# Second layer's x: from TensorE's 128x128 transposes to VectorE's 32x32 blocks and scattering transfers

## What is computed

```
def hybrid_layer(x, w_in, a_group_w, a_scale, b_sinks, c_rel_bias, w_out, ln_gain, ln_bias):
    h = jnp.einsum('bsd,de->bse', x, w_in)
    a_v, a_gate, b_q, b_k, b_v, b_gate, c_q, c_k, c_v, c_gate = jnp.split(h, _split_points(), axis=-1)
    a_out = pool_mixer(a_v, a_group_w, a_scale) * jax.nn.silu(a_gate)
    b_out = swa_sink_attention(b_q, b_k, b_v, b_sinks) * jax.nn.silu(b_gate)
    c_out = chunk_relbias_attention(c_q, c_k, c_v, c_rel_bias) * jax.nn.silu(c_gate)
    mix = jnp.concatenate([a_out, b_out, c_out], axis=-1)
    y = jnp.einsum('bse,ed->bsd', mix, w_out)
    return _layer_norm(DEEPNORM_ALPHA * x + y, ln_gain, ln_bias)

def reference(x, ...):
    for l in range(DEPTH):
        x = hybrid_layer(x, w_in[l], a_group_w[l], ...)
    return x
```

## Time and profile before

| | |
|---|---|
| median of three runs | 2855.98 us |
| the profiled execution's own time | 2856.79 us |
| its span in the profile | 2854.9 us |
| TensorE (PE) busy | 2833.2 us, 99% |
| VectorE (DVE) busy | 1727.1 us, 60% |
| ScalarE (ACT) busy | 1305.9 us, 46% |
| GpSimd (POOL) busy | 1250.3 us, 44% |
| DMA | 364.43 MB, 128 GB/s in the mean |

### The profile page before, as it was taken

The page is one execution under the profiler, slowest core; times in us unless marked ns, Lnnn a source line. Parts: engine busy times, 40 slices in busy tenths (PEclk is TensorE's granted clock), DMA queues, the critical chain, the costliest instruction groups (busy, mean ns, idle before and its releaser), DMA issues.

```text
span 2854.9 us, 45183 instructions
## 1 busy us (share of the span) xinstructions
PE 2833.2 (99%) x13520; PEld 2373.2 (83%) x13520; DVE 1727.1 (60%) x2898; ACT 1305.9 (46%) x2711; POOL 1250.3 (44%) x926
## 2 busy tenths in 40 slices
PE   8999999999999999999999999999999999999998
PEld 7888888888888888888888888888888888888886
DVE  5555579623666777861166666895127667678624
ACT  4444466523444445652244444664234444456521
POOL 4444444444344434444444444444444444444441
PEclk9999999999999999999999999999999999999999
DMA  6333222355444422235554443224454444222442
GB/s 197 123 122 122 94 86 83 103 175 182 143 144 143 144 85 86 88 98 168 167 167 152 148 148 95 84 82 137 145 180 138 141 144 143 86 85 81 137 156 103
DMA packets 189168, 364.43 MB, mean 128 GB/s; under 512 B 18912, under 2 KB 27136, under 8 KB 185344
## 3 DMA queue, kind: packets, MB, share of 16 engines
q1 hardware_dynamic: 185264, 347.25, 38.2%
q10 hardware_dynamic: 3792, 15.73, 1.4%
HBM read 320.94 MB, written 45.11 MB: 128 GB/s over the span
## 4 chain that ended last, share of the span: by engine, by line
PE 99%; DVE 0%; DMA 0%; SPq 0%; issue 0%; ACT 0%; POOL 0%; POOLq 0%
PE acc L555 69%; PE sc L555 17%; PE pv L555 9%; PE sc L616 2%; PE sc L653 1%; PE sc L579 0%; PE acc L585 0%; DMA raw<-in_wall 0%; PE acc L579 0%; PE sc L591 0%; PE pv L579 0%; DVE last_sums L1777 0%; DVE last_sums L1776 0%; SPq L419 0%; POOL wl L1289 0%
## 5 line engine op out<-in xcount | busy, mean ns | idle before, releaser
L1289 POOL TENSOR_TENSOR wl<-raw,wh 128x512 fp32r<-128x512 f32 x920 | 1249.6, 1361 | 1560.8 <-ACT wh L914 1557.9
L555 PE MATMUL acc<-xh,wh 128*128 128x512 f32 x2624 | 1036.8, 395 | 9.6 <-DVE xl L1322 9.6
L914 ACT ACTIVATE wh<-raw 128x512 fp32r<-128x512 f32 x920 | 575.4, 630 | 1020.1 <-PE acc L555 696.0
L555 PE MATMUL acc<-xh,wl 128*128 128x512 f32 x2624 | 1024.6, 390 | 0.0
L555 PE MATMUL acc<-xl,wh 128*128 128x512 f32 x2624 | 1024.4, 390 | 0.0
L555 PEld LDWEIGHTS acc<-xh,wh 128*128 128x128 f32 x2624 | 494.3, 188 | 105.2 <-issue 6.6
L555 PEld LDWEIGHTS acc<-xh,wl 128*128 128x128 f32 x2624 | 493.5, 188 | 105.6
L555 PEld LDWEIGHTS acc<-xl,wh 128*128 128x128 f32 x2624 | 494.8, 189 | 94.4
L555 PE MATMUL sc<-wh,mixh 128*128 128x512 f32 x496 | 195.2, 394 | 0.1
L555 PE MATMUL sc<-wh,mixl 128*128 128x512 f32 x496 | 193.2, 390 | 0.0
L555 PE MATMUL sc<-wl,mixh 128*128 128x512 f32 x496 | 193.0, 389 | 0.0
(11 more groups left out here) (227 smaller groups left out, 3568.8 us busy)
## 6 DMA issues: line engine op xcount, KB each, us to landing
raw<-in_wall SPq DMA_DIRECT2D x920, 256.0 KB, 2.6
res_scratch<-res ACTq DMA_DIRECT2D x12, 1024.0 KB, 4.3
res<-res_scratch SPq DMA_DIRECT2D x12, 1024.0 KB, 4.9
res<-in_x SPq DMA_DIRECT2D x8, 1024.0 KB, 5.8
x_scratch<-res SPq DMA_DIRECT2D x8, 1024.0 KB, 4.7
prob<-x_scratch SPq DMA_DIRECT2D x32, 256.0 KB, 3.3
res<-x_scratch SPq DMA_DIRECT2D x8, 1024.0 KB, 5.8
hist_scratch<-mixh SPq DMA_DIRECT2D x8, 768.0 KB, 4.5
```

What stands on the lines that cost most here:

```text
L555: return nc.tensor.matmul(o, lhsT, rhs, start=start, stop=stop)
L914: return nc.scalar.activation(o, i, ACT.Copy, scale=scale)
L1289: nc.gpsimd.tensor_tensor(wl[:, s, :], raw[:, s, :], wh[:, s, :].bitcast(F32), ALU.subtract).then_inc(w_lo, 1)
```

## The change

VectorE turns the normalised quarter, still in SBUF, in blocks of 32x32 (`turn_rows`, behind the keys' low parts and ahead of the queries'), into four buffers `turned` that lie over four tiles of `mixh` and `mixl` which only p = 3 fills. SyncE writes these as columns into a new scratch array `x1_t` of 2048 x 1024 (`store_turned`): for each of the units 20 to 23 four transfers ahead of the unit's load, each of 32 partitions x 16 blocks x 32 elements. A run of 32 elements is 128 bytes, and its neighbours in the transfer lie in other rows of `x1_t`. ScalarE waits for all 16 transfers of p before it writes `mixh` behind the last `c_hi`. The plain store into `x1` stays, since the residual is read from it. In the output projections of steps 1 and 2 the pieces are loaded from `x1_t` as step 0 loads them from `x_t`; TensorE's 128 transposes and their waits are gone, and ScalarE and VectorE read `prob` in SBUF.

```diff
+        x1_t = nc.dram_tensor("x1_t_scratch", (D, SEQ), F32, kind="Internal").ap()
...
+        turned = [nc.alloc_sbuf_tensor_at(f"turned{n}", [P, HALF], F32, offset=x_at + 4 * HALF * (at + tile + C_PAIRS - 1))
+                  for n, (at, tile) in enumerate((a, b) for a in (2 * KT, 3 * KT) for b in (MIX_A, MIX_C))]
...
+        def turns(it):
+
+            return 1 <= it <= 2
...
+            sp.sem_inc(turned_out, 16)
...
+            def store_turned(it, n, t):
+
+                sp.wait_ge(turned_ok, n * QT + (16 * it + t + 1))
+                for i in range(4):
+                    at = half(it) * HALF + t * P + 32 * i
+                    sp.dma_start(x1_t.rearrange("(n j a) s -> n a j s", n=4, a=32)[ds(n, 1), :, :, at:at + 32]
+                                 .rearrange("o a j b -> (o a) j b"),
+                                 turned[t][32 * i:32 * (i + 1), :].rearrange("a (j b) -> a j b", b=32)
+                                 ).then_inc(turned_out, 16)
...
                         if s == 20 and it:
                             store_ln(it - 1, p)
+                        if 20 <= s and turns(it):
+                            store_turned(it - 1, p, s - 20)
...
-                            sp.wait_ge(*x_taken(it, m * 8 + gg - 1))
-                            if layer(it + 1) == 0:
-                                src = x_t.rearrange("(k p) n -> k p n", p=P)[ds(m * 8 + gg, 1), :, HALF:2 * HALF]
-                            else:
-                                src = x_rows(it + 1).rearrange("(t p) (k n) -> t k p n", p=P, n=512)
-                                src = src[ds(2 * m + gg // 4, 1), gg % 4]
+                            sp.wait_ge(xl_ok, m * 8 + (16 * (it + 1) + gg - 1))
+                            if turns(it):
+                                sp.wait_ge(turned_out, 1024 * it + 16)
+                            src = (x_t if layer(it + 1) == 0 else x1_t).rearrange("(k p) n -> k p n", p=P)
+                            src = src[ds(m * 8 + gg, 1), :, half(it + 1) * HALF:(half(it + 1) + 1) * HALF]
...
-            def transpose_x(g, bank):
-
-                for b in range(4):
-                    last = nc.tensor.transpose(bank[:, b * P:(b + 1) * P], prob[:, g % 2, b * P:(b + 1) * P], ident[:])
-                last.then_inc(tr_full, 1)
...
-                            if u in X_AT and 2 <= it + 1:
-                                gg = X_AT.index(u)
...
-                                transpose_x(gg, (odd_banks, even_banks)[n][gg % 4])
...
                     c_hi(it, p, 3)
+                    if turns(it):
+                        act.wait_ge(turned_out, p * 256 + (1024 * (it - 1) + 256 + 16))
                     mix_hi(p * 2 + (nb + 1), p + MIX_A)
...
+            def turn_rows(it, n):
+
+                dv.wait_ge(ln_ok, n + (4 * it + 1))
+                dv.wait_ge(turned_out, n * 256 + (1024 * it + 16))
+                for t in range(QT):
+                    V.transpose(turned[t][:], res[:, t, :]).then_inc(turned_ok, 1)
...
                     keys_lo([k[:, HALF:2 * HALF] for k in ck_l], acc[0], [k[:, HALF:2 * HALF] for k in ck]).then_inc(k_ok, 1)
+                    if turns(it):
+                        turn_rows(it - 1, p)
                     queries_lo(cq, acc[1], SCALE, p * 2 + 2 * pc)
```

More of the change, by code:

```diff
@@ L264, in build @@
         x0_in = [sem(f"x0_in{k}") for k in range(KT)]
-        tr_full = sem("tr_full")
+        turned_ok = sem("turned_ok")
+        turned_out = sem("turned_out")
         xh_ok = sem("xh_ok")
@@ L557, in _ @@
             pe.sem_inc(w_used, RING)
-            pe.sem_inc(tr_full, 2)
             def project(it, r, q, bank, slot, part=range(4), x_first=False):
@@ L825, in _ @@
                         banks = (even_banks, odd_banks)[n]
[L826 to L829, removed]
                         if n:
@@ L942, in x_hi_tile @@
                 copy(xh[:, ds(tile, 1), :].rearrange("p o n -> p (o n)"), source).then_inc(xh_ok, 1)
[L944 to L949, removed]
             for q in range(4):
@@ L1243, in _ @@
                             gg = X_AT.index(s)
[L1244 to L1248, removed]
+                            act.wait_ge(xin[gg % 2], m * 64 + (128 * it + 16 * (gg // 2 + 1)))
+                            x_hi_tile(m * 8 + gg, prob[:, gg % 2, 0:512])
                         if m == 0 and s < U_N:
@@ L1335, in queries_lo @@
                                            q[h][ROWS[h], :].bitcast(F32), ALU.mult, ALU.subtract).then_inc(q_ok, 1)
[L1337 to L1340, removed]
             def gate_ready(n, bank):
@@ L1701, in _ @@
                         for gg in range(4 * n, 4 * n + 4):
[L1702 to L1707, removed]
+                            dv.wait_ge(xh_ok, m * 8 + (16 * (it + 1) + gg + 1))
+                            o, hi = (v[:, ds(m * 8 + gg, 1), :].rearrange("p o n -> p (o n)") for v in (xl, xh))
+                            lo(o, prob[:, gg % 2, 0:512], hi).then_inc(xl_ok, 1)
                         c = 2 * m + n
```

## The result

| | median | lowest to highest | runs |
|---|---|---|---|
| before | 2856.39 us | 2855.89 to 2856.70 | 7 |
| after | 2865.91 us | 2864.59 to 2866.46 | 7 |

The ratio is 1.0033, with a 95% interval of 1.0024 to 1.0042. The profiled execution took 2864.59 us, 1.3 us less than the median.

The account below looks back on a forecast made before the run. The prediction took TensorE, busy 99% of the span, as the bound. 2856.8 - 15.3 (transposes) + 77.8 (late loads) + 18 (clock) = 2937.3 us, given as 2937 us for the median; range 2870 to 3110 us.

Parts of the forecast that it names:

- Removed: Output projections of steps 1 and 2: without TensorE's transposes, 7.64 us less a step, -15.3 us in all.
- VectorE's block transposes: Four for each p, 3.0 us taken, hidden in VectorE's 5.60 us gap between keys and queries: 0 us.
- rival D: VectorE late if one block transpose exceeds 1.4 us; at 2.5 us each, 35 us more; chance 0.05.
- The price of a packet: SyncE's scattering transfers: 37 ns for each 128-byte packet, from landings of two 1 MB stores; ends 5.5 and 87.5 ns.
- +77.8 us: TensorE's loss from late unit 23 loads: 13.5 us in each p of step 2, 5.95 in each of step 1.
- Rival B: Scattering transfers: a short write costs about twice as much, 73.5 ns a packet, 3088 us in all; chance 0.22.
- The issue time is shorter than the drain and hidden by it: SyncE's queue: issuing 16 transfers takes 7 us in a p, less than their packets' time, so adds nothing.
- the drain: DMA engines working off the short packets ahead of unit 23's load: 512 packets of 37 ns, 18.8 us.
- The place and the chain: Steps 1 and 2: unit 23's late load delays ScalarE's conversion, the probabilities' parts and TensorE's scores; 14.75 us late in step 2.
- Rival C: Cheap packet, 5.5 ns: issues bound the queue, hist transfers 7 us later, 2.6 us lost, 2843 us; chance 0.13.
- break-even of 17.7 ns: Packet price at which TensorE's loss from the scattering transfers equals the 15.3 us gain.
- TensorE's clock: Slower clock behind TensorE's gaps: 3 us for each p of step 2, half in step 1, +18 us (ends 0 and 40).

Follow-up runs that it names:

- e1: Changed kernel without block transposes, scattering transfers and their waits; layer 2 reads the input's transposed x, so works on wrong data: 2841.28 us.
- e5: Changed kernel with plain stores of the turned rows, the 128-byte runs gathered when pieces of x are loaded in the output projections: 2841.69 us.
- e8: Changed kernel with runs of 64 bytes in the 16 transfers of each p, same issues and bytes, twice the packets, wrong layer 2 data: 2887.88 us.
- e3: Changed kernel with one transfer per unit 20 to 23 instead of four, 2048 runs of 32 bytes each, a quarter of the bytes: 2848.41 us.
- e2: Changed kernel with the same 16 transfers per p and same bytes, but runs of 2 KB, 32 packets a transfer instead of 512: 2861.15 us.

## Why the prediction was wrong in size

**Removed: right.** -15.3 us from the windows; both projections fell to 184.84 us, and e1 alone gives 14.9.

**VectorE's block transposes: right.** 0.67 us each, 0.74 taken. Four stand in the gap that was named, and 3.08 us of its 5.60 are left; the timeline of VectorE in the changed kernel, p = 1 of step 2 (start, duration, in brackets the idle time before):

```profile
1539.69 2.50 DVE L1478 STREAM_TRANSPOSE turned<-res 128x512 f32<-128x512 f32 x4
1545.26 0.68 DVE L1319 SCALAR_TENSOR_TENSOR mixh<-acc,mixh 64x512 fp32r<-64x512 f32 x1 [3.08 <-ACT mixh L907]
```

e5 keeps the transposes and loses nothing, so rival D falls.

**The price of a packet: this step failed.** 37 ns was taken, from two stores of 1 MB that differ by 24 packets an engine; the runs bound it to 12 or 13 ns (e8, e3), and the busy shares give about 5 ns for a further packet with the same bytes, where the prediction had 33. On it rest the +77.8 us of the sum: TensorE's idle time is 14.3 us, all of it in step 2. The difference between the two landings was put down to the number of packets, but each is the time of one transfer by itself, not the rate of a stream, and the stores stand in different stretches of the program; which of the two misled was not tested. The landings of the small transfers would have been too high as well: with 2, 32 and 64 packets an engine they are 1.9, 2.3 and 2.9 us (e2, after, e8), 13 and 19 ns for each further packet. Rival B, twice the price for a short write, falls as well.

**"The issue time is shorter than the drain and hidden by it": the wrong way round.** For a group the drain is at most 128 x 13 ns + 0.7 = 2.4 us and the issue 2.9. With the right price the sum would have used the issue: the hist transfers issued at 11.2, plus the 6.8 us that the prediction's own terms give for them and a load (4.2 + 0.7 + 1.9). That is 18.0 us, 5.0 late, less 1.2 to spare: 3.8 us for each p of step 2; the load was seen at 18.6, and 3.3 us of idle time. For step 1 the load is issued at 10.9 and lands, by the 2.7 us of the profile's page, at 13.6, ahead of its turn at 16.35: nothing lost, and the trace shows nothing.

**The place and the chain: right for step 2.** Units 20 to 23, `wh`, `pt`, scores, in this order. For step 1 23.8 us were forecast and none came. Rival C had the mechanism of what happened (bound by the issues, the hist transfers pushed back) and forecast a loss of 0.65 us a p. It pushed the hist transfers back by 7 us, at 0.45 us an issue, where 9.2 were seen (11.2 - 1.9), and its unit 23 landed at 14.8 and not 18.6; its other terms are not given, so the rest of that difference can't be placed. It also counted nothing for the clock. Its break-even of 17.7 ns rests on the drain and says nothing here. The range was cut above it, so that it stood outside, and that the direction came true is no credit to the drain.

**TensorE's clock: the mechanism right, the size too large.** 18 us was taken. In the changed kernel the clock was below 1.00 behind three of the four gaps of 3 us and never in step 1, where there are no gaps. A window at p = 1, where it stayed at 1.00, and one at p = 2, where the mean of 8 us was 0.57, between the two levels of 1.2 and 2.4 GHz (same columns):

```profile
1560.00:1565.00 5.00, 1.85 (x10) 1.33 (x9) 1.46 (x4) 2.18 (x5) 1.42 (x2) 1.00 0.76 252
...
1640.00:1648.00 8.00, 6.04 (x17) 5.27 (x18) 5.56 (x14) 4.12 (x10) 2.56 (x2) 0.57 0.49 165
```

Read in windows of 1 us, the clock was at 0.50 for some 3, 6 and 3 us behind these gaps and cost 6.2 us in all. 14.3 us idle and 6.2 us by the clock leave 2.4 of the 22.9 us. The idle time counts from the modelled end of a matmul, 0.39 us behind its start where the next could start after 0.227, so each of the 8 waits can cost 0.16 us more than it shows, 1.3 us in all; the last 1.1 us are open.

The Trainium skill's rule in "DMA: Bandwidth & Descriptors", section "Why small descriptors are slow (HBM only)", was set aside on the strength of the two landings. The bounds of 12 and 13 ns from e8 and e3 are nearer to it than to the 37 ns that was taken: by its 7 cycles against 67, and 87.5 ns for a packet of 2 KB, an estimate from that page is 9 ns. What the same page's "Specifications" say of transfers under 512 bytes did not show as a price: writes of 128 bytes were no bottleneck.

## What to carry to other kernels

Before pricing the bytes or packets of transfers that are put in front of others in a queue, count their issues: here 16 x 0.55 us of SyncE's time moved 1.5 MB into the path of one weight load. All of it cost 25 us against a gain of 15, and 20 of the 25 stayed when 61,440 of the short packets were taken away. Take a rate from a stream of transfers, never from the difference of two landings. And ask not only how much a transfer costs but what hangs on the load behind it: the same packets cost nothing in the output projections, where ScalarE waits for no weight load, and the version that sorts on the load (2841.7 us) beats both kernels.

## What the hardware showed that was not expected

- A scattered store with runs of 128 bytes, each in another row of DRAM, lands in 2.3 us for 64 KB, where the same bytes in runs of 2 KB take 1.9 us (e2). In a stream of runs of 64 bytes a packet costs at most 12 ns of each engine's time (e8).
- The issue of one transfer on SyncE takes 0.35 us with 512 runs, but 0.58 us with 1024 and 0.60 us with 2048 (e8, e3).
- TensorE's clock fell to 0.50 of full speed, 1.2 GHz, behind idle times of 3.75, 3.14 and 3.14 us (p = 0, 2 and 3 of step 2) and stayed at 1.00 behind one of 3.15 us (p = 1).
